# Loading two expert pieces per layer earlier, and dealing the slot-number products out over up products

## What is computed

```
for i in range(4):
    hc, hl = modulated rmsnorm of xc, xl
    yc, yl = mixer_i(hc), mixer_i(hl)          # ends with  (...) @ w_out
    xc, xl = xc + gc1 * yc, xl + gl1 * yl
    x = concat(modulated rmsnorm of xc, xl)     # 256 rows
    sel = sigmoid(x @ router_w) + router_b      # best group, then best 2 of its 4 experts
    hid = silu(x @ wg[e]) * (x @ wu[e])         # for the rows of expert e
    y   = sum_e combine[:, e] * (hid @ wd[e])
```

## Time and profile before

| | |
|---|---|
| median of three executions | 1925.81 us |
| the profiled execution | 1928.63 us |
| its span in the trace | 1926.8 us |
| PE busy | 1794.3 us (93%) |
| DVE, ACT, POOL busy | 25%, 20%, 2% |
| mean rate of the DMAs | 316 GB/s |
| TensorE clock granted, mean | 0.962 of full |

### The profile page before, as it was taken

How to read it: one execution, slowest core, us unless ns; L and a number is a source line. 1 busy time by engine, 2 the same in 40 slices (tenths; PEclk the granted TensorE clock), 3 DMA queues, 4 the chain that set the end, 5 groups by cost and what they waited for, 6 DMA issues and landing times.

```text
span 1926.8 us, 21722 instructions
## 1 busy us (share of the span) xinstructions
PE 1794.3 (93%) x8848; PEld 1060.3 (55%) x8848; DVE 478.3 (25%) x1238; ACT 387.7 (20%) x763; POOL 40.7 (2%) x52
## 2 busy tenths in 40 slices
PE   4999999989998979999989997999998999999976
PEld 2678544346636858734436565854434778444443
DVE  0243411015200341411102434231111343211102
ACT  1232200013103660200002223210001342000002
POOL 1000000000000000000000000000000000000000
PEclk8999899999999989999999998999999999999988
DMA  9977899996997232799998884489999457899960
GB/s 322 360 290 303 322 426 428 426 411 246 356 358 257 90 126 93 280 411 426 427 427 296 314 314 179 167 331 426 428 427 407 159 218 277 348 427 426 428 272 22
DMA packets 134022, 609.47 MB, mean 316 GB/s; under 512 B 12485, under 2 KB 19277, under 8 KB 108960
## 3 DMA queue, kind: packets, MB, share of 16 engines
q1 hardware_dynamic: 116880, 589.32, 76.9%
q10 hardware_dynamic: 12528, 10.70, 1.8%
q0 software_dynamic: 4512, 8.02, 1.1%
HBM read 606.15 MB, written 8.92 MB: 319 GB/s over the span
## 4 chain that ended last, share of the span: by engine, by line
PE 77%; DMA 14%; DVE 3%; ACT 3%; issue 2%; ACTq 1%; DVEq 0%; SPq 0%; POOLq 0%
PE PS L926 21%; PE PS L1468 18%; PE PS L1479 9%; DMA arena<-in_moe_wu 7%; PE PS L1432 6%; DMA arena<-in_moe_wg 6%; PE PS L956 4%; PE PS L1008 3%; PE PS L976 2%; PE PS L1412 1%; DMA ring<-in_w_mod 1%; PE PS L1445 1%; PE PS L994 1%; DVE RS L1606 1%; PE PS L1454 1%
## 5 line engine op out<-in xcount | busy, mean ns | idle before, releaser
L1468 PE MATMUL PS<-ring,arena 128*64 128x512 f32 x1312 | 395.7, 607 | 17.3 <-DMA arena<-in_moe_wu 9.6
L1468 PEld LDWEIGHTS PS<-ring,arena 128*64 128x64 f32 x1312 | 126.6, 140 | 213.2 <-issue 213.2
L857 ACT ACTIVATE arena<-PS 128x512 f32<-128x512 f32 (+2 forms) x131 | 71.5, 546 | 830.9 <-PE PS L1459 331.2
L1980 DVE TENSOR_TENSOR arena<-arena,PS 128x512 f32<-128x512 f32 x32 | 33.5, 1047 | 592.9 <-PE PS L1468 592.9
L926 PE MATMUL PS<-HS,ring 128*128 128x256 f32 x768 | 173.7, 384 | 4.7 <-ACT arena L716 3.0
L1468 PE MATMUL PS<-arena 128*64 128x512 f32 x576 | 173.9, 602 | 1.2 <-DMA arena<-in_moe_wg 1.2
L926 PEld LDWEIGHTS PS<-HS,ring 128*128 128x128 f32 x768 | 144.6, 191 | 31.3 <-issue 9.2
L1432 PE MATMUL PS<-arena 128*128 128x256 f32 (+3 forms) x688 | 143.8, 364 | 9.4 <-ACT arena L857 4.3
L1479 PE MATMUL PS<-ring,arena 128*64 128x512 f32 x656 | 148.8, 595 | 0.5 <-DVE arena L1961 0.5
L926 PE MATMUL PS<-arena,ring 128*128 128x256 f32 (+1 forms) x672 | 145.6, 377 | 2.3 <-ACT arena L646 1.1
L1432 PEld LDWEIGHTS PS<-arena 128*128 128x128 f32 (+1 forms) x688 | 117.6, 194 | 50.5 <-issue 22.7
(11 more groups left out here) (328 smaller groups left out, 1709.7 us busy)
## 6 DMA issues: line engine op xcount, KB each, us to landing
ring<-in_w_mod SPq DMA_DIRECT2D x48, 2048.0 KB, 16.3
ring<-in_moe_wu SPq DMA_DIRECT2D x41, 2048.0 KB, 18.2
ring<-in_moe_wd SPq DMA_DIRECT2D x41, 2048.0 KB, 22.0
ring<-in_moe_wg SPq DMA_DIRECT2D x41, 2048.0 KB, 23.3
arena<-in_moe_wg SPq DMA_DIRECT2D x24, 2048.0 KB, 19.7
HS<-in_moe_wu SPq DMA_DIRECT2D x12, 2048.0 KB, 18.9
arena<-in_moe_wu SPq DMA_DIRECT2D x12, 2048.0 KB, 22.3
arena<-in_moe_wd SPq DMA_DIRECT2D x12, 2048.0 KB, 27.0
```

The costliest lines, as they stand in the source:

```text
L857: A(dst, src, func).then_inc(S(sem), 1)
L1468: ins = mm(PS[64 * e:64 * e + 64, b, :], XG[:, k, 64 * e:64 * e + 64], w[:, k], start=(k == 0), stop=(k == KD - 1))
L1980: tt(by_k(HID), row(SG), row(bank(here[1])), ALU.mult).then_inc(S("hid"), 1)
```

## The change

Four things are changed.

1. The two arena pieces (q = 0 and 1) are issued before ring piece q = 7 in layer 0, 5 in layer 1, 7 in layer 2 and 3 in layer 3, and no longer after the mixer's last residual add. In layer 1 SP waits there for `l_hn` 16 and `out` 80, in layer 2 for `g_kt` 2. The third spare piece still waits for `ht`.
2. To free the arena rooms, intermediates move: `MP` to 8000, the mLSTM's gated output to `mHN`, which is `mQK`, `gSO` to 6144, and `gOG` to the place of `gR`.
3. In the GLA mixer ACT's copies into `gOG` (L833) go. DVE reads the head outputs from PSUM, after the square (`g_hq`), and the products that reuse these banks wait for DVE (`g_og`).
4. `slot_id` takes one pair's number and issues its two products. It is called behind each of the first seven steps of the second `up` of pair 0. `slot_id` (the semaphore) now rises behind the seventh step; the wait for `onehot` stands before that `up`.

```
+                def early():
+                    if l == 1:
+                        sp.wait_ge(S("l_hn"), 16)
+                        sp.wait_ge(S("out"), 80)
+                    if l == 2:
+                        sp.wait_ge(S("g_kt"), 2)
+                    load(n)
+                    load(n + 1)
                 for q in range(SPARE, SPARE + RING):
+                    if q == (7, 5, 7, 3)[l]:
+                        early()
                     load(n + q)
-                sp.wait_ge(S("x"), KD * (2 * l + 2))
-                sp.wait_ge(S("out"), (32, 80, 112, 144)[l])
-                for q in range(SPARE):
-                    if q == SPARE - 1:
-                        sp.wait_ge(S("ht"), 4 * (l + 1))
-                    load(n + q)
+                sp.wait_ge(S("ht"), 4 * (l + 1))
+                load(n + SPARE - 1)
...
-                    run(A(gOG[:, 2 * h:2 * h + 2], v, ACT.Copy), "g_os")
...
-                    pe.wait_ge(S("g_hq"), i + 1)
+                    pe.wait_ge(S("g_og"), 2 * i + 2)
...
-                def slot_id():
-                    pe.wait_ge(S("onehot"), 2 * (l + 1))
-                    for p in range(1, NPAIR):
-                        for s in range(2):
-                            ins = mm(bank(3, p, p + 1), OH[...], c_("tid")[:, s:s + 1], ...)
-                    ins.then_inc(S("slot_id"), 1)
+                def slot_id(p):
+                    for s in range(2):
+                        ins = mm(bank(3, p, p + 1), OH[...], c_("tid")[:, s:s + 1], ...)
+                    if p == NPAIR - 1:
+                        ins.then_inc(S("slot_id"), 1)
...
-                def up(ws, b, sem, ready=None):
+                def up(ws, b, sem, ready=None, ids=False):
                     for k in range(KD):
...
+                        if ids and k < NPAIR - 1:
+                            slot_id(k + 1)
...
-                        up(ws, here[g], "up", 2 * n + 2 if g == 0 else None)
-                        if first and g == 0:
-                            slot_id()
+                        if first and g == 1:
+                            pe.wait_ge(S("onehot"), 2 * (l + 1))
+                        up(ws, here[g], "up", 2 * n + 2 if g == 0 else None, ids=(first and g == 1))
```

More of the change, by code:

```diff
@@ L300, in program @@
         ROOM = [ring[:, r].rearrange("p a b -> p (a b)") for r in range(RING)] + [arena[:, 9608 + 4096 * e:13704 + 4096 * e] for e in range(2)] + [HS[:, :].rearrange("p a b c -> p (a b c)")]
-        MP = [ar(16000, 512), ar(16000, 512), ar(12288, 512), ar(15360, 512), ar(16000, 512)]
+        MP = [ar(8000, 512), ar(8000, 512), ar(12288, 512), ar(15360, 512), ar(8000, 512)]
         QT = ar(0, 8, N2)
@@ L323, in program @@
         mRM = ar(16384, 3, N2)
+        mHN = mQK
         mRAW = sq(0, 4, N2)
@@ L352, in program @@
         gAT = ar(15360, 8, T)
-        gOG = ar(10240, 8, N2)
-        gSO = ar(13312, 8, 256)
+        gOG = gR
+        gSO = ar(6144, 8, 256)
         gKD = ar(8192, 8, T)
@@ L1292, in mlstm @@
                                 pe.wait_ge(S("l_hn"), 16)
-                            ins = group(bank(m, 0, N2), zip(tile(w, m), [mO[:, 8 * r + k] for k in range(KD)]), None, first=(r == 0), final=(r == 1))
+                            ins = group(bank(m, 0, N2), zip(tile(w, m), [mHN[:, 8 * r + k] for k in range(KD)]), None, first=(r == 0), final=(r == 1))
                             if r:
@@ L1447, in turn_x @@
                             ins.then_inc(S(sem), 1)
-                def slot_id():
-                    pe.wait_ge(S("onehot"), 2 * (l + 1))
-                    for p in range(1, NPAIR):
-                        for s in range(2):
-                            ins = mm(bank(3, p, p + 1), OH[:, s, p].rearrange("t y n -> t (y n)"), c_("tid")[:, s:s + 1], start=(s == 0), stop=(s == 1))
-                    ins.then_inc(S("slot_id"), 1)
+                def slot_id(p):
+                    for s in range(2):
+                        ins = mm(bank(3, p, p + 1), OH[:, s, p].rearrange("t y n -> t (y n)"), c_("tid")[:, s:s + 1], start=(s == 0), stop=(s == 1))
+                    if p == NPAIR - 1:
+                        ins.then_inc(S("slot_id"), 1)
                 def turn_w(b, sem, rows=P):
@@ L1794, in gated @@
                         v.wait_ge(S("l_zt"), m // 2 + 1)
-                        run(stt(mO[:, m], bank(4 + m // 2 % 4, N2 * (m % 2), N2 * (m % 2) + N2), prm("mg", 1, m), mO[:, m], ALU.mult, ALU.mult), "l_hn")
+                        run(stt(mHN[:, m], bank(4 + m // 2 % 4, N2 * (m % 2), N2 * (m % 2) + N2), prm("mg", 1, m), mO[:, m], ALU.mult, ALU.mult), "l_hn")
                 masks(0)
@@ L1880, in gla @@
                 for m in range(8):
-                    v.wait_ge(S("g_os"), m // 2 + 1)
-                    run(stt(gOG[:, m], gOG[:, m], prm("gg", 1, m), gR[:, m], ALU.mult, ALU.mult), "dve")
+                    v.wait_ge(S("g_hq"), m // 2 + 1)
+                    run(stt(gOG[:, m], bank(m // 2, N2 * (m % 2), N2 * (m % 2) + N2), prm("gg", 1, m), gR[:, m], ALU.mult, ALU.mult), "g_og")
                 after(v, "g_root")
```

## The result

The changed kernel takes 1961.5 us, the median of four executions (1952.9 to 1967.9), against 1925.0 for the kernel before (four executions, 1918.6 to 1926.3). The ratio is 1.018, with a 95% interval of 1.0147 to 1.0213: 36.6 us slower. Forecast were 1964 us, in a range of 1942 to 1978, and slower by more than 0.5% with a chance of 0.85.

A forecast was written before the change was run, and what follows sets the result against it. TensorE (PE) was taken to bound the kernel, busy 1794.3 of 1926.8 us. Gather wait 31.0, clock 8.0 and mixer -0.6 gave +38.4 us: 1967.0 on the profiled execution, 1964 against the median, range 1942 to 1978.

The forecast's parts named there:

- The wait on the gather: In pair 0, later slot numbers delay the gather; PE idles about 8 us a layer, `turn_x` later by 31.0 us in all.
- E: The end of the first `up` of pair 0, from which the prediction counts its times in each layer.
- I take 10.3: Assumed flight of pair 0's gather in us, between the layer's 8.8 and the full queue's 11.0; bounds 7.9 and 12.2.
- The products on PE: Second `up` of pair 0: steps with two products take 1.56 us, last slot number at E + 10.9, clock expected to stay.
- rival A: The clock falls in the dealt-out `up` too: 2.5 us a layer, +10, so 1974 us; chance 0.08.
- The clock after the wait: Behind PE's idle time on the gather the clock is low: 2.0 us a layer, 8 us in all (bounds 0 and 10.2).
- The stream shifts with PE: SP's issues hang on the `down` of pair 0, behind the gather, so the end of the layer gives nothing back.
- rival B: The layer's tail absorbs the wait, up to 30.8 us: +7.6, 1933 us, not tellably slower; chance 0.08.
- The early pieces: Two arena pieces issued earlier: 0 us, since the first `up` has no wait and full rooms make the DMA wait.
- The GLA mixer: ACT's copy of 0.60 us per head goes, only the last head's on the path: -0.6 us (bounds 0 and -2.5).
- Rival C: The gather lands fast, in 2.9 us, as the queue before it is emptier: about 1926 us, no change; chance 0.04.
- The 3.2 us: Skill's time for a 512 KB DMA issued by GpSimd, 2.0 us plus bytes / 436e3; by it almost no loss, 61.7 against 59.2.

The follow-up runs named there:

- Dealing alone: The kernel before with only the one-column products dealt out behind seven steps of the second `up`: 1961.3 us, ratio 1.0194.
- behind three steps: The changed kernel with the seven pairs of one-column products behind the first three steps of the second `up` (3, 3, 1): 1921.1 us, ratio 0.9986.
- `turn_x` behind `down`: The changed kernel with `turn_x` of pair 0 and its wait for the gather moved behind the `down` of pair 0: 1931.2 us, ratio 1.0044.
- two pieces held back: The changed kernel with SP issuing piece 11 and all behind it only when the gather for pair 1 has landed: 1941.2 us, ratio 1.0064.
- early pieces alone: The changed kernel with the one-column products back in one block between the two `up` of pair 0: 1925.4 us, ratio 1.0004.
- three steps, 64 columns: The changed kernel with the products behind three steps, each moving 64 equal columns in place of one: 1917.9 us, ratio 0.9967.
- the same kernel again: The version with three steps, 64 columns and the early pieces, measured once more: 1918.5 us, ratio 0.9959.
- three steps, no early pieces: The kernel before with the one-column products behind three steps, without the early pieces and the GLA edit: 1922.2 us, ratio 0.9996.
- block, 64 columns: The kernel before with its block of 14 products between the two `up`, each moving 64 equal columns: 1929.5 us, ratio 1.0022.

## Why the prediction was right

**The wait on the gather: right, and it is the loss.** Forecast were slot numbers at E + 10.9, the gather's issue at E + 12.2, its landing at E + 22.55, an idle PE of about 8 us a layer and a flight of 10.3 us. With E = 204.78 + 7.02 = 211.80, layer 0 shows 222.48 = E + 10.7, 223.80 = E + 12.0, 234.79 = E + 23.0, waits of 7.6 to 8.4 us and a flight of 10.95. Over the four layers `turn_x` starts 33.9 us later than before (forecast 31.0), since the flights took 11.0 to 11.8 us. Dealing alone gives the whole loss, and moving only the waiting instruction takes 30 us of it back. But "I take 10.3" isn't a property of the gather: it is its flight beside the two pieces, and without them it is 3.5 to 4.3.

**The products on PE: right.** A group of two with an `up` step takes 0.54 + 1.01 = 1.55 us, forecast 1.56. The clock stays at 1.00 in it, so rival A (the clock falls in the dealt-out `up`) is out.

**The clock after the wait: right in size, incomplete in cause.** `turn_x` and `down` take 1.97 + 7.98 = 9.95 us. At full clock they take 1.09 + 7.02 = 8.11, by the chain of the version behind three steps. That is 1.8 us in layer 0, 7.4 in all four; forecast 2.0 and 8.0. With no gather wait at all (`turn_x` behind `down`) the clock was low there too, behind the wait for the silu. I had left that wait out: ACT stands until the last slot number is there, so `turn_h` waits 1.0 us longer than before. It added nothing to the sum, as it lies ahead of the wait on the gather.

**"The stream shifts with PE": the step that was mis-sized.** Pair 0 lost 41.3 us (forecast 39.0). I took the stretch from pair 0 to pair 7 as unchanged, rival B as up to 30.8 us shorter. It became 10.4 us shorter: PE's idle time in it fell from 31.0 to 23.6 us, and the mean granted clock rose from 0.989 to 0.993, which is worth about 3 us more. The DMA is busy all through it (share 1.00 to 1.01, 420 to 423 GB/s), so its length goes with what is left to move: 323.6 MB before, 316.7 in the changed kernel. But this isn't the wait being absorbed, for the stretch is as short in kernels whose pair 0 is hardly longer than before, or shorter. What goes with it is how long before the end of `down` the pieces 11 and 12 are issued (sums of four layers; `down` of pair 0 to `down` of pair 7):

| kernel | piece 11 issued ahead of the end of `down`, us | pair 0, us | pair 0 to 7, us |
|---|---|---|---|
| two pieces held back | 8.9 to 10.4 | 128.1 | 766.1 |
| early pieces alone | 9.9 to 10.6 | 117.9 | 766.2 |
| before | 9.9 to 10.7 | 117.4 | 764.2 |
| three steps, 64 columns | 10.6 to 12.8 | 115.3 | 762.5 |
| the same kernel again | 11.0 to 12.9 | 118.7 | 756.5 |
| three steps, no early pieces | 10.8 to 12.8 | 115.9 | 757.3 |
| block, 64 columns | 11.8 to 14.9 | 121.6 | 755.6 |
| dealing alone | 21.0 to 23.0 | 159.9 | 755.6 |
| changed | 21.1 to 21.9 | 158.7 | 753.8 |

Above about 11 us the stretch stays near 756 us, and the further 10 us of the changed kernel bring little or nothing, less than the 6 us by which two executions of one kernel differ. I read it so, without a run that isolates it: two pieces that land before `down` ends leave the stream nothing to catch up, and a second `up` at full clock, which lets go of their rooms sooner, is enough for that. The layers are 30.9 us longer and the two profiled executions differ by 27.7; the other 3 us lie in the mixers, within their spread from run to run (9 us between two executions of one kernel). The changed kernel's median is 5 us over its profiled execution, which brought the total near the forecast: part of the closeness of 1961.5 to 1964 is chance. From profile to profile the forecast was +38.4 us and the result +27.7.

**The early pieces: right** as far as the runs can tell: nothing beside the block, with the reservation above for the other arrangements. **The GLA mixer: right**, 0.6 us on ACT.

**Rival C and the page.** The 3.2 us, an estimate by the fit of the Trainium skill ("DMA: Bandwidth & Descriptors", section "Anatomy of one DMA — SWDGE (gpsimd) path"), are close to the gather without the two pieces, 3.48 us in layer 0 and up to 4.3 in the others. I set the figure aside since none of 28 landed under 7.5 us. None of the four first gathers before had an empty queue: an older piece landed 8.4 to 9.6 us after the gather's issue. So rival C failed on its condition: the gather did not meet an emptier queue.

## What to carry to other kernels

Before work is dealt out over a longer stretch to hide it, look at who waits for its last result. Here it was a gather whose landing had 0 to 1.5 us to spare, and 7 us of lateness a layer cost 37 us in four. A small transfer on the critical path should be issued while few large prefetches are under way: 3.5, 6 or 11 us for the same 512 KB. Holding the prefetches back for it has its price, though: that version stayed slower than the kernel before (ratio 1.0064). And before time that the clock gives back is counted as a gain, look at what else is due right behind it: with the 64-column block PE came sooner and waited 6.8 us for the gather.

## What the runs showed of the hardware

Flight of the first gather of layer 0 (128 rows of 4 KB), by when it starts:

| kernel | the two pieces of 2 MB next to it, issued | the second landed after the gather's issue, us | flight, us |
|---|---|---|---|
| two pieces held back | 12.0 and 11.6 us before | 1.4 | 3.5 |
| behind three steps | 7.6 and 7.2 us before | 5.6 | 6.1 |
| before | 5.3 and 4.9 us before | 8.6 | 8.8 |
| block, 64 columns | 4.6 and 4.2 us before | 9.2 | 9.4 |
| changed | 0.3 us before, and 0.1 us after | 13.9 | 11.0 |

In the three middle rows the gather lands 0.2 to 0.5 us behind the second piece. In the changed kernel it lands between the two (the first after 8.3 us).

A product with a 128x128 stationary operand that moves 1 column is hardly cheaper than one that moves 64: six of them behind an `up` step took 1.43 us with one column and 1.48 with 64 (layer 0 of the three-step versions), and the block of 14 took 3.28 us with 64 columns and 3.49 to 4.00 us with one. What differs in the block is TensorE's clock behind it. With one column the next `up` took 9.57 us in place of 7.02, at a granted clock of 0.52; with 64 columns the clock stayed at 1.00.
